# A transformer pair on one core: eight units of the first expert up stage as full fp32 products, and the gate groups started earlier and spread thinner

## The reference, cut to what matters

```
q = (t @ wq).reshape(T, 8, 2, 128)
s1, s2 = q[:, :, 0] . k1, q[:, :, 1] . k2            # scores against 128 keys each
v1, i1 = top_k(s1, 16);  v2, i2 = top_k(s2, 16)
cand = v1[..., :, None] + v2[..., None, :]           # 256 candidates a head
sc, pos = top_k(cand, 16);  idx = i1 * 128 + i2 at pos;  g = softmax(sc)
act = gelu(einsum('thkd,td->thk', u[idx], t))
out = einsum('thk,thkd->td', g * act, v[idx])
```

## Time and profile before

| | us |
|---|---|
| median of 3 runs | 3056.58 (3055.95 to 3056.8) |
| span of the profiled execution, first to last instruction | 3054.2 |
| PE busy, share | 3004.1, 98% |
| DVE busy, share | 2268.2, 74% |
| ACT busy, share | 1409.3, 46% |
| POOL busy, share | 186.1, 6% |
| last matmul of the third unit of u0 starts | 547.36 |
| last gate group starts | 736.51 |

### The profile page before, as it was taken

How to read it: one execution, slowest core, us unless ns; L and a number is a source line. 1 busy time by engine, 2 the same in 40 slices (tenths; PEclk the granted TensorE clock), 3 DMA queues, 4 the chain that set the end, 5 groups by cost and what they waited for, 6 DMA issues and landing times.

```text
span 3054.2 us, 49503 instructions
## 1 busy us (share of the span) xinstructions
PE 3004.1 (98%) x19430; PEld 2799.9 (92%) x19430; DVE 2268.2 (74%) x3252; ACT 1409.3 (46%) x1718; POOL 186.1 (6%) x233
## 2 busy tenths in 40 slices
PE   8999999999999999999999999999999999999998
PEld 8899889999999999999999999999788888888887
DVE  5777559999768988888888877698656646555564
ACT  4464443466445454545454456434445333333333
POOL 1000000020001111111111000000000000000000
PEclk9999999999999999999999999999999999999999
DMA  5443454466668999999999874544444555555554
GB/s 209 178 139 138 157 205 173 166 234 231 237 252 313 358 352 356 351 349 343 359 342 350 317 280 166 194 166 161 157 172 167 185 192 190 191 183 191 192 186 159
DMA packets 102147, 705.59 MB, mean 231 GB/s; under 512 B 13016, under 2 KB 13040, under 8 KB 18464
## 3 DMA queue, kind: packets, MB, share of 16 engines
q1 hardware_dynamic: 78272, 562.07, 50.5%
q0 software_dynamic: 21872, 128.10, 11.9%
q10 hardware_dynamic: 1872, 13.63, 1.1%
HBM read 685.46 MB, written 18.24 MB: 230 GB/s over the span
## 4 chain that ended last, share of the span: by engine, by line
PE 87%; DVE 9%; ACT 2%; issue 1%; DMA 1%; SPq 0%; POOL 0%; POOLq 0%; ACTq 0%; DVEq 0%
PE bank L2018 29%; PE bank L2019 15%; PE bank L2048 7%; PE bank L2050 7%; PE bank L2049 7%; PE bank L1996 6%; PE bank L1997 6%; PE bank L1998 6%; PE bank L2024 2%; DVE raw_lo L1163 2%; DVE split L1163 1%; DVE pick_a L1624 1%; ACT split L713 1%; PE bank L2115 1%; DVE pick_b L1619 1%
## 5 line engine op out<-in xcount | busy, mean ns | idle before, releaser
L2018 PE MATMUL bank<-a_both,split 128*128 128x416 f32 (+1 forms) x3840 | 1222.5, 376 | 2.3 <-DVE split L1163 1.9
L1163 DVE TENSOR_TENSOR raw_lo<-raw,split 128x2048 fp32r<-128x2048 f32 x292 | 668.6, 2290 | 390.2 <-ACT split L713 387.1
L713 ACT ACTIVATE split<-raw 128x2048 fp32r<-128x2048 f32 x308 | 588.6, 1911 | 487.8 <-DMA raw<-stream_dram 308.1
L2018 PEld LDWEIGHTS bank<-a_both,split 128*128 128x128 f32 x3840 | 721.1, 188 | 55.8 <-issue 5.9
L2019 PE MATMUL bank<-a_both,split 128*128 128x208 f32 x3072 | 762.0, 258 | 0.0
L2019 PEld LDWEIGHTS bank<-a_both,split 128*128 128x128 f32 x3072 | 584.6, 190 | 0.9
L1996 PE MATMUL bank<-a_both,split 128*128 128x256 f32 (+1 forms) x1984 | 572.5, 289 | 12.0 <-DVE raw_lo L1163 6.8
L1163 DVE TENSOR_TENSOR split<-raw,split 128x2048 fp32r<-128x2048 f32 x240 | 549.6, 2290 | 33.0 <-ACT split L713 11.0
L729 ACT ACTIVATE split<-raw 128x1536 fp32r<-128x1536 f32 x224 | 333.8, 1490 | 505.3 <-PE bank L2019 501.3
L1997 PE MATMUL bank<-a_both,split 128*128 128x256 f32 (+1 forms) x1984 | 560.4, 282 | 0.0
L1998 PE MATMUL bank<-a_both,raw_lo 128*128 128x256 f32 (+1 forms) x1728 | 488.8, 283 | 0.0
(11 more groups left out here) (344 smaller groups left out, 3071.0 us busy)
## 6 DMA issues: line engine op xcount, KB each, us to landing
raw<-stream_dram SPq DMA_DIRECT2D x532, 1024.0 KB
gates_scratch<-stage ACTq DMA_DIRECT2D x13, 1024.0 KB, 4.3
gbuf<-gates_scratch POOLq DMA_DIRECT2D x30, 416.0 KB, 6.9
x<-x_dram SPq DMA_DIRECT2D x4, 512.0 KB, 7.1
x_scratch<-x POOLq DMA_DIRECT2D x1, 2048.0 KB, 11.4
mem<-mem_dram POOLq DMA_DIRECT2D x1, 2048.0 KB, 9.5
xm<-x_scratch POOLq DMA_DIRECT2D x1, 2048.0 KB, 12.1
out_dram<-x SPq DMA_DIRECT2D x4, 512.0 KB, 3.0
```

The lines of the kernel that those rows point to most:

```text
L713: eng.activation(high(k, is_near(k))[:, :], raw[:, k % RAW, :], ACT.Copy).then_inc(hi_done, 1)
L1163: eng.tensor_tensor(low(k, is_near(k)), raw[:, k % RAW, :], high(k, is_near(k))[:, :].bitcast(F32), ALU.subtract).then_inc(split_done, 1)
L2018: mm(o, hi[:, ks], pair, start=kt == 0, stop=False)
```

## The change

Eight units of u0 (its units 3 to 10, the list `WHOLE`) are no longer split. PE multiplies them from the raw slot as plain float32 against `a1_whole`, the sum of the two parts of the activations, which POOL makes with four additions of 128 x 4 x 208 after it has issued the write of `xw`. `splits(k)` replaces `k + 1` in all waits on `split_done`, since eight signals fall away. The stages u0 and u1 are now one loop of 32 units s, wholly in the far scheme; NEAR0 is the first unit of e0. Gate groups begin in unit s = 12, with two; then three in odd and four in even units, until the last group, alone in unit 27. On DVE the list `waiting` holds only the four splits of the units 11 to 14, one of them inside the index steps, two after the softmax and the last within the gate groups.

```diff
+        a1_whole = at("a1_whole", [P, KT, T], F32, x_at)
+        GATES_FROM = 12
+        GATES_STEP, _n = {}, 0
+        for _s in range(GATES_FROM, 32):
+            _k = 2 if _s == GATES_FROM else 4 - _s % 2
+            GATES_STEP[_s] = list(range(GROUPS))[_n:_n + _k]
+            _n += _k
+        LAST_GROUP = max(s for s, groups in GATES_STEP.items() if groups)
-        NEAR0, NEAR1 = UNIT0["u1"], UNIT0["ck"]
+        NEAR0, NEAR1 = UNIT0["e0"], UNIT0["ck"]
+        WHOLE = [UNIT0["u0"] + j for j in range(3, 11)]
+        def splits(k):
+            return k + 1 - sum(w <= k for w in WHOLE)
...
+            eng.wait_ge(tmp_split, BQ["ln2"] + 16)                       # POOL
+            for c in range(4):
+                ks = slice(4 * c, 4 * c + 4)
+                eng.tensor_tensor(a1_whole[:, ks, G:T], a1[0][:, ks, G:T].bitcast(F32), a1[1][:, ks, G:T].bitcast(F32),
+                                  ALU.add).then_inc(whole_done, 1)
...
+            for s in range(32):                                          # ACT
+                u, groups = UNIT0["u0"] + s, GATES_STEP.get(s, [])
+                for q in groups:
                     evict_group(q)
                 eng.wait_ge(mm_done, u + 1)
+                if s == 0:
+                    ahead(u)
+                eng.activation((act0 if s < 16 else act1)[:, s % 16, 0:TD], bank[s % 4][:, 0:TD], ACT.Gelu).then_inc(bank_free, 1)
+                if s > 0:
+                    ahead(u)
+                if s in (6, 8):
+                    gate_exp((s - 6) // 2)
...
-            waiting = [UNIT0["u0"] + j for j in range(16)]
+            waiting = [u for u in range(UNIT0["u0"], UNIT0["u0"] + GATES_FROM) if next_unit(u) not in WHOLE]
...
+            for s in range(GATES_FROM, LAST_GROUP + 1):                  # DVE
+                for n, q in enumerate(GATES_STEP[s]):
+                    if n == min(2, len(GATES_STEP[s]) - 1):
+                        ahead(UNIT0["u0"] + s - 1)
                     picks(q)
...
+            for s in range(LAST_GROUP, 32):                              # DVE, after gated0(0)
+                ahead(UNIT0["u0"] + s)
+                if s == LAST_GROUP:
                     gated0(1)
...
+            def whole_unit(j, between):                                  # PE
+                o = bank[j % 4][:, 0:TD]
+                for kt in range(KT):
+                    last = mm(o, raw[:, j % RAW, kt * P:kt * P + P], a1_whole[:, kt, G:T], start=kt == 0, stop=kt == KT - 1)
+                    if kt == KT - 1:
+                        last.then_inc(mm_done, 1)
+                    between(kt)
```

More of the change, by code:

```diff
@@ L928, in _, with gate_exp @@
                     ahead(UNIT0["wq"] + s)
-            def gelu0(g, j):
-                eng.activation(act0[:, g * 4 + j, 0:TD], bank[j][:, 0:TD], ACT.Gelu).then_inc(bank_free, 1)
             eng.wait_ge(s_xw, 16)
[L934 to L941, removed]
+            def gate_exp(tt):
+                eng.wait_ge(sm_dve, tt + 1)
+                eng.activation(sc[:, tt, :, :], sc[:, tt, :, :], ACT.Exp).then_inc(sm_act, 1)
             def evict_group(q):
@@ L1167, in ahead @@
                 k = next_unit(u)
-                if k is not None:
-                    lo(lin(k + 1, *loops), k)
+                if k is not None and k not in WHOLE:
+                    lo(lin(splits(k), *loops), k)
             def split_pair(dst, kt, src, sig, ap=None):
@@ L1583, in _ @@
                 for half in range(2):
-                    if waiting:
+                    if (tt, half) == (1, 1):
                         fill()
@@ L1811, in _ @@
             widen(3)
-            lo(NEAR1 + NEAR + 1, NEAR1 + NEAR)
+            lo(splits(NEAR1 + NEAR), NEAR1 + NEAR)
             means()
@@ L2262, in out1_unit @@
                 c, k = OUT1_ORDER[j]
[L2263 removed]
+                eng.wait_ge(split_done, splits(UNIT0["out1"] + j))
                 if k == 0:
@@ L2342, in gate_group, with between @@
                         .then_inc(g_mm, 1)
-            for k in range(16):
-                groups = GATES_UNIT.get(k, [])
-                places = GATES_AFTER if k else GATES_AFTER[-len(groups):]
-                def between(kt, groups=groups, places=places):
+            def whole_unit(j, between):
[5 more added lines that the diff above has]
+                    between(kt)
+            for s in range(32):
+                u, groups = UNIT0["u0"] + s, GATES_STEP.get(s, [])
+                def between(kt, groups=groups, places=GATES_AFTER if s > GATES_FROM else GATES_AFTER[-len(groups):]):
                     if kt in places and places.index(kt) < len(groups):
                         gate_group(groups[places.index(kt)])
-                eng.wait_ge(split_done, UNIT0["u1"] + k + 1)
-                eng.wait_ge(bank_free, 4 * ROUND0["u1"] + k + 1)
-                if k == 0:
+                if u in WHOLE:
+                    if u == WHOLE[0]:
+                        eng.wait_ge(whole_done, 4)
+                    eng.wait_ge(raw_full[u % RAW], 16 * (u // RAW + 1))
+                else:
+                    eng.wait_ge(split_done, splits(u))
+                eng.wait_ge(bank_free, 4 * ROUND0["u0"] + s + 1)
+                if s == GATES_FROM:
                     picks_turn()
-                feature_unit(k, a1, between=between, c0=G, near=True)
+                if u in WHOLE:
+                    whole_unit(u, between)
+                else:
+                    feature_unit(u, a1, between=between, c0=G)
             feature("e0", 16, None, unit=part_unit, tile=e0_pair, c1=TD, ready=lambda kt: eng.wait_ge(a2_ready, Z_TILES + kt + 1))
@@ L2467, in mix2_unit @@
             def mix2_unit(s):
-                eng.wait_ge(split_done, UNIT0["vg"] + s + 1)
+                eng.wait_ge(split_done, splits(UNIT0["vg"] + s))
                 if s < 32:
@@ L2504, in _ @@
                 c = j // 4
-                eng.wait_ge(split_done, UNIT0["out2"] + j + 1)
+                eng.wait_ge(split_done, splits(UNIT0["out2"] + j))
                 if j % 4 == 0:
@@ L2561, in _ @@
             for j in range(4):
-                eng.wait_ge(split_done, u0 + j + 1)
+                eng.wait_ge(split_done, splits(u0 + j))
                 eng.wait_ge(bank_free, 4 * r0 + 2 * j + 2)
@@ L2583, in _ @@
                 c = (j // 4) % 2
-                eng.wait_ge(split_done, UNIT0[down] + j + 1)
+                eng.wait_ge(split_done, splits(UNIT0[down] + j))
                 if j % 4 == 0:
```

55 lines of the change are left out of this document (17 added, 38 removed).

## The result

| | us |
|---|---|
| before, median of 11 runs | 3056.84 (3055.95 to 3060.81) |
| after, median of 11 runs | 3064.01 (3061.03 to 3066.96) |
| ratio, 95% interval | 1.0021 [1.0013, 1.0029] |
| span of the profiled execution, before and after | 3054.2, 3058.9 |

The changed kernel is slower by 0.21%, 6.4 us by the ratio and 7.2 by the medians; the two profiled executions are 4.7 us apart. The forecast was 3060.4, in a range of 3049 to 3067.

A forecast was written before the change was run, and what follows sets the result against it. PE, busy 98% of the span, bounds the kernel, so only gaps and half clock can be won. Removed 21.7 us, added 25.5, net +3.8 on 3056.58 gives 3060.4 us; range 3049 to 3067.

The forecast's parts named there:

- u0: gaps and clock gone, whole units: Units 3 to 10: 8.3 us of gaps and half clock go; whole units add 2.0, format changes 0.2.
- gaps before groups: Eleven PE gaps before gate groups, 4.4 us shown, 7.3 in all with DVE the bound; removed by spreading the groups.
- behind the last group: u1 after the last gate group: PE's 3.2 us wait for a split plus 2.9 at half clock, 6.1 removed.
- late third groups, units 13 to 26: Third gate groups wait for DVE rows: +2.0 at unit 13, +12.5 over units 14 to 26, +1.1 at block ends.
- unit 27: Its only gate group stands behind a split: +4.8 us, then +2.9 for the clock falling behind the gap.
- POOL's additions: Four additions beside wq, 0.8 to 2 us each, costed at nothing; up to 2 us with DVE's 2.39 idle gone.
- Rival D: Whole units cost the unscaled 256-column record, +10 us over the forecast, 3070; chance 0.04.
- The chain of latencies: Gated units: ACT's hi copy, DVE's split, then third-group rows; PE loses 0.86 us a unit, plus 0.1 paced group.
- Rival B: Third groups aren't late, as copies and splits run further ahead; 15.6 us less than forecast, 3044.8; chance 0.19.
- rival C: Clock falls at recurring third-group gaps, units 13 to 26, about 1.7 us each; six falls give 3070.6; chance 0.10.
- E: Clock doesn't fall at unit 27, or its gap is shorter: 3057.5 down to 3052.7; 0.55 together with the forecast.
- rival F: Split of unit 30 or of e0 late behind gate loads: +3 to +6 us, 3065; 0.12 with POOL's lock.

The follow-up runs named there:

- e10: e5 with POOL's four additions set apart, one by one, as in e7; 3046.0 us, ratio to before 0.9966.
- e8: Changed kernel with the edits of e3 and e7 together; 3038.91 us, ratio to before 0.9941.
- e9: Kernel before, with u1 put in the far scheme and nothing else; 3050.81 us, ratio to before 0.998.
- e3: Changed kernel, with DVE making each unit's split after the rows of all its gate groups instead of before the third; 3042.12 us, ratio 0.9948.
- e11: e10 with DVE's split after the rows of all five gate groups; 3042.78 us, ratio to before 0.9954.
- e1: Changed kernel run again, unedited; 3063.57 us, ratio to before 1.0020.
- e2: Changed kernel without POOL's additions; whole units read only the hi part of the activations; 3062.34 us, ratio to before 1.0014.
- e7: Changed kernel with POOL's four additions set apart, each waiting for the split of one more pair of wq units; 3059.51 us, ratio to before 1.0011.
- e5: Changed kernel with gate groups back at their old places, five a unit from unit 16; whole units and far scheme kept; 3047.04 us, ratio 0.9969.

## Why the prediction was right, step by step

Net at unit 31 (last column) the changed kernel is 6.0 us later than the one before; the forecast's terms made 3.8.

| term | forecast | measured, from |
|---|---|---|
| u0: gaps and clock gone, whole units | -6.1 (-8.3 + 2.2) | -6.11: s=2 to 10, 51.14 to 45.03 |
| gaps before groups | -7.3 | -7.30: e10 to e8, s=31 |
| behind the last group | -6.1 | -6.13: before to e9, s=26 to 31 |
| late third groups, units 13 to 26 | +15.6 (2.0 + 12.5 + 1.1) | +15.29: s=12 to 26, after to e8 |
| unit 27 | +7.7 (4.8 + 2.9) | +6.69: s=26 to 27, after to e8 |
| POOL's additions | 0 | +3.55: s=2, before to after |
| sum | +3.8 | +5.99 (the last column itself: +6.02) |

- **Whole units.** 5.63 us each, 0.176 a record, against 5.61 forecast by scaling the 256-column rows. Rival D is out.
- **The chain of latencies.** Gaps of 0.71 shown before each third group, ended by `pick_a`, units of 9.0 and 9.9 us, one gap of 4.51 before the last group: all as written. Rival B (3044.8) would have needed the calls in another order, and that is what e3 is: with it the kernel runs at 3042.1. So 22 of the 25 us between the changed kernel and the best one hang on the place of one call, which cost 2.1 us with five groups a unit (e10 to e11) and 22 with three and four.
- **The clock.** Over 600 to 740 us it was granted at 1.00 through all those gaps, so rival C is out. Behind the 4.51 us gap it fell to the 1.2 GHz level, as forecast, but cost 1.9 us (6.7 less the 4.8 of the gap) and not the 2.9 of the nearest row. The same gap in e1, e2 and e7 cost 2.4, 2.1 and 2.2 by the same reckoning, so this price isn't fixed even for one kernel. E (no fall) is out. The units behind it are 5.36 us apart, so no split was late behind the gate loads (rival F).
- **Behind the last group.** The 6.1 us went, but not because the last group came to stand elsewhere. They belong to the far scheme, which prepares u1 a unit further ahead, and which I had costed at nothing with only a loss to fear. The prediction's steps lean on that distance (the split of unit 30 made while the units 28 and 29 are still to come) but don't name it as the cause. With the size right and the edit wrong, the sum held, which is luck; the expectation of e5, built on it, missed by 7 us.
- **POOL's additions: the step that failed.** I cost them at nothing, and at up to 2 us with the cover gone. They took 3.55. The terms together missed by 2.2 only because unit 27 was priced 1.0 too high and the third groups 0.3. The arithmetic is in the rows: the split beside them was 6.34 us longer, DVE had 0.41 and 2.39 us of idle before its next two splits to absorb that (the splits at 461.58 and 468.22 of e7; the earlier trace rows has the second), and 6.34 - 2.80 = 3.54 was pushed through the full top-k to PE, which waited for splits at the end of wq and in the first units of u0, and from there to the end. I had the second cover right (2.39) and the thing to be covered wrong: what counted was one DVE operation that made next to no headway beside all 7.8 us of POOL's work.

The rows show first that POOL's four additions kept their pace (1.95 us each, against 1.98 alone in e7), while the DVE operation with two SBUF inputs ended a little less than its own length after the last of them: they ran one after the other. The Trainium skill, "SBUF — State Buffer", section "SBUF: two separate sides", states just such an exclusive lock, held for a whole instruction. The trace agrees, with one difference: by the rule as I applied it, the split waits for the addition under way (0.6 us here) and the next addition waits for the split; here the split waited through all four, which stand back to back. No run here shows whether a pause between them would have let it in earlier than their end.

The span (+4.7) is less than the table (+6.0) by 0.2 at its start and 1.1 behind unit 31; the medians (+7.2) are more. Neither difference has a cause that a run here shows; both are within what repeated runs of one kernel show. The measured 0.21% stands at the border of the 0.2% by which the forecast told no change from slower, and the 7.2 us of the medians are nearly twice its 3.8.

## What to carry to other kernels

When work is taken off an engine that is the bound, look next at the order of its calls: a wait inside its program that cost little under the old load (2.1 us here) can cost far more under the new one (22), for with the bound gone it is the latency through that wait that other engines see. Test each edit of a change alone, also those that were made only to let the others in: here one of these (the far scheme, one constant) brought 6 us by itself and hid a loss of the others. And an operation put on an idle engine isn't free because that engine is idle: look at which operation of the others stands beside it in time.

## What the runs showed of the hardware

- An addition of 832 columns with two inputs took POOL 1.95 to 1.99 us. Four of them back to back held up a DVE subtraction with two SBUF inputs for 6.34 us; a single one beside `MAX8` steps (0.87 and 0.74 us) left the durations of both engines as they were.
- Gaps of 0.71 us every 9 to 10 us left the clock at 1.00. Behind a gap of 4.51 us a window showed 0.59 and the loss was 1.9 to 2.4 us in four runs; behind one of 7.23 us a window of 7 us showed 0.50 and the loss was 3.0 us.
- A plain float32 unit of 208 columns took 5.63 us, the same unit as three fp32r products 5.36. Two records instead of three cost 5% in time and spare ACT and DVE their copy and split.
